# Expert rows added to the residual in DRAM by indirect transfers, in place of gathered rows added on VectorE

## What is computed

```python
h2 = rmsnorm(x, norm2_g[l])
x = x + hier_moe(h2, ...)    # top-1 group of 4, then top-2 experts of the 4 in it
# in hier_moe, for every expert e:  y = y + (silu(t @ w_gate[e]) * (t @ w_up[e]) * gate[:, e]) @ w_down[e]
```

## Time and profile before

| | us |
|---|---|
| median of 3 runs | 1093.71 (1092.78 to 1094.87) |
| the profiled execution | 1096.58 |
| its span, first to last instruction | 1094.3 |
| around the span | 2.3 |
| PE busy | 1034.2 (95%) |
| DVE busy | 549.2 (50%) |
| ACT busy | 291.3 (27%) |
| POOL busy | 191.8 (18%) |

### The profile page before, as it was taken

The page is one execution under the profiler, slowest core; times in us unless marked ns, Lnnn a source line. Parts: engine busy times, 40 slices in busy tenths (PEclk is TensorE's granted clock), DMA queues, the critical chain, the costliest instruction groups (busy, mean ns, idle before and its releaser), DMA issues.

```text
span 1094.3 us, 26585 instructions
## 1 busy us (share of the span) xinstructions
PE 1034.2 (95%) x11288; PEld 765.1 (70%) x11288; DVE 549.2 (50%) x1264; ACT 291.3 (27%) x570; POOL 191.8 (18%) x265
## 2 busy tenths in 40 slices
PE   8999998899999999899989999989999999998894
PEld 7875874587689977586578577646876778764552
DVE  5899996524711111020679999764364112102018
ACT  6225336623000100000342443465230001000013
POOL 3400000000223442322200000000003335332230
PEclk9999999999999999999999999999999999999997
DMA  9652211153999999999934122011569999999993
GB/s 358 209 230 78 77 58 39 39 193 147 394 399 406 402 404 401 405 402 400 345 125 137 53 93 89 20 51 50 202 261 401 403 406 400 404 401 407 396 389 127
DMA packets 85109, 279.07 MB, mean 255 GB/s; under 512 B 12344, under 2 KB 12448, under 8 KB 84976
## 3 DMA queue, kind: packets, MB, share of 16 engines
q1 hardware_dynamic: 69504, 237.60, 56.8%
q0 software_dynamic: 15472, 39.63, 9.8%
HBM read 257.43 MB, written 22.54 MB: 256 GB/s over the span
## 4 chain that ended last, share of the span: by engine, by line
PE 64%; DVE 16%; DMA 10%; issue 3%; ACT 3%; SPq 3%; DVEq 0%; ACTq 0%
PE ps L861 20%; PE ps L901 9%; DVE arena L1620 7%; PE ps L459 7%; PE ps L461 7%; PE ps L460 7%; DMA deep<-in_w_dn 3%; DMA deep<-in_w_gu 3%; SPq L410 3%; DVE w_lo L440 2%; PE ps L906 2%; DMA arena<-in_w_dn 2%; DVE x_sb L1559 2%; DMA arena<-in_w_gu 2%; PE ps L1048 2%
## 5 line engine op out<-in xcount | busy, mean ns | idle before, releaser
L1839 DVE SCALAR_TENSOR_TENSOR arena<-ps,gslot,arena 128x128 f32<-128x128 f32 x88 | 25.7, 345 | 368.1 <-ACT arena L1259 333.2
L861 PE MATMUL ps<-arena 128*32 128x256 f32 x2112 | 129.6, 380 | 6.3 <-DMA arena<-in_w_dn 3.2
L640 POOL DMA_INDIRECT gain<-h_rows,tab x82 | 85.1, 1037 | 231.6 <-DVE arena L1831 188.9
L459 PE MATMUL ps<-a_hi,w_hi 128*128 128x512 f32 (+1 forms) x304 | 122.5, 403 | 3.1 <-DVE w_lo L440 2.1
L460 PE MATMUL ps<-a_lo,w_hi 128*128 128x512 f32 (+1 forms) x304 | 119.3, 392 | 0.0
L461 PE MATMUL ps<-a_hi,w_lo 128*128 128x512 f32 (+1 forms) x304 | 119.2, 392 | 0.0
L861 PEld LDWEIGHTS ps<-arena 128*32 128x32 f32 x2112 | 90.4, 110 | 39.2 <-issue 9.7
L861 PE MATMUL ps<-deep,arena 128*32 128x256 f32 x1824 | 106.6, 379 | 1.0 <-DMA deep<-in_w_dn 1.0
L861 PE MATMUL ps<-raw,arena 128*32 128x256 f32 x1696 | 103.2, 379 | 0.5
L435 ACT ACTIVATE w_hi<-raw 128x1024 fp32r<-128x1024 f32 (+1 forms) x64 | 65.0, 1022 | 131.1 <-PE ps L461 130.9
L1259 ACT ACTIVATE arena<-ps 128x384 f32<-128x384 f32 (+1 forms) x32 | 14.9, 465 | 315.3 <-PE ps L861 248.8
(11 more groups left out here) (266 smaller groups left out, 1511.7 us busy)
## 6 DMA issues: line engine op xcount, KB each, us to landing
arena<-in_w_gu SPq DMA_DIRECT2D x92, 512.0 KB
deep<-in_w_gu SPq DMA_DIRECT2D x84, 512.0 KB
raw<-in_w_gu SPq DMA_DIRECT2D x80, 512.0 KB
raw<-in_w_dn SPq DMA_DIRECT2D x56, 512.0 KB
deep<-in_w_dn SPq DMA_DIRECT2D x44, 512.0 KB
raw<-in_w_in SPq DMA_DIRECT2D x40, 512.0 KB
arena<-in_w_dn SPq DMA_DIRECT2D x28, 512.0 KB
raw<-in_w_out SPq DMA_DIRECT2D x16, 512.0 KB
```

The costliest lines, as they stand in the source:

```text
L459: nc.tensor.matmul(o, lh, rh, start=start, stop=False)
L640: pool.indirect_dma_start(xg[:, s * QC:(s + 1) * QC], None, h2q[l], bass.IndirectOffsetOnAxis(ap=tab[:, s, e:e + 1], axis=0), bounds_check ...
L861: mm = T.matmul(o, rows, piece[:, :, c * P:(c + 1) * P], start=b == 0, stop=b == 7)
L1839: ins = V.scalar_tensor_tensor(out=slu[:, s, :], in0=hidden(e, 1)[:, s, :], scalar=gslot[:, s, e:e + 1], in1=slu[:, s, :], op0=ALU.mult, o ...
```

## The change

The DRAM buffer in slot order is no longer used for the stored places. A DRAM buffer per layer in token order, `xsum`, takes its part. POOL stores each tile of the mixed x into it, ahead of the tile of h2. For each stored place POOL issues an indirect DMA per group of 32 slots (three, or two for a light place), which adds the 128 quarter rows of `ysb` to the rows of `xsum` that `tab` names; an empty slot's index is out of bounds. Before a place's additions it waits until those of the place before have landed. At the end four plain DMAs load the sums over x. The late additions, their eight indirect gathers, the index steps in `extras` and eleven of the twelve zero stores are gone. The places 14 and 15 go as before.

```diff
@@ zero stores, layer 0
-                    for tile in range(1 + EXTRA):
-                        pool.dma_start(yd[ZERO_ROW + tile * P:ZERO_ROW + (tile + 1) * P, :], zeros).then_inc(y_zero, 16)
+                    pool.dma_start(yd[ZERO_ROW:ZERO_ROW + P, :], zeros).then_inc(sums_begun, 16)
@@ mixing phase, for each tile tt
+                    pool.wait_ge(x_mixed, 8 * l + 2 * (tt + 1))
+                    pool.dma_start(xsum[l][tt * P:(tt + 1) * P, :], x[:, tt, :]).then_inc(sums_begun, 16)
                     pool.wait_ge(hrow_set, 4 * k + tt + 1)
                     pool.dma_start(h2d[l][tt * P:(tt + 1) * P, :], hrow[:, tt, :]).then_inc(h2_stored, 16)
@@ def store(e)
                     pool.wait_ge(y_set, STORED * l + e + 1)
-                    rows = yd[FIRST_ROW[e]:FIRST_ROW[e + 1], :].rearrange("(s i) (c n) -> c i s n", i=G, c=4)
-                    for c in range(4):
-                        pool.dma_start(rows[c], ysb[G * c:G * c + G, 0:GROUPS_OF[e] * QC].rearrange("i (s n) -> i s n", n=QC)).then_inc(y_stored, 16)
+                    if e:
+                        pool.wait_ge(y_stored, 16 * stored(l, e))
+                    else:
+                        pool.wait_ge(sums_begun, 16 * (1 + TT * (l + 1)))
+                    for s in range(GROUPS_OF[e]):
+                        pool.indirect_dma_start(xsq[l], bass.IndirectOffsetOnAxis(ap=tab[:, s, e:e + 1], axis=0), ysb[:, s * QC:(s + 1) * QC], None,
+                                                bounds_check=4 * SEQ - 1, oob_is_err=False, compute_op=ALU.add).then_inc(y_stored, 16)
@@ after the last store
-                if l == 0:
-                    pool.wait_ge(y_zero, 16 * (1 + EXTRA))
-                pool.wait_ge(y_stored, 64 * STORED * (l + 1))
+                pool.wait_ge(y_stored, 16 * stored(l, STORED))
                 for tt in range(TT):
-                    for k in range(TOPE):
-                        q = TOPE * tt + k
-                        if q == LATE_FREE:
-                            pool.wait_ge(w_used, (l + 1) * PIECES_L - 8)
-                        pool.indirect_dma_start(late_rows[q], None, yd,
-                                                bass.IndirectOffsetOnAxis(ap=yidx[:, 0, k, tt:tt + 1], axis=0)).then_inc(yc_in[tt], 16)
+                    pool.dma_start(x[:, tt, :], xsum[l][tt * P:(tt + 1) * P, :]).then_inc(x_back[tt], 16)
@@ SP, ahead of the second group of projection weights of layer 1
-                            sp.wait_ge(yc_in[TT - 1], 32 * l)
+                            sp.wait_ge(x_back[TT - 1], 16 * l)
@@ DVE
-            def add_late(l, tt):
-                ve.wait_ge(yc_in[tt], 32 * (l + 1))
-                for k in range(TOPE):
-                    ve.wait_ge(late_add, TOPE * (TT * l + tt) + k)
-                    V.tensor_tensor(x[:, tt, :], late_rows[TOPE * tt + k], x[:, tt, :], ALU.add).then_inc(late_add, 1)
             def sum_ready(l, tt):
-                ve.wait_ge(late_add, TOPE * (TT * l + tt + 1))
+                ve.wait_ge(x_back[tt], 16 * (l + 1))
                 ve.wait_ge(ysum_ready, TT * l + tt + 1)
@@ DVE, extras(l): the twelve steps that made yidx[:, 0] are removed
@@ DVE, end of a layer
                     last_y(l, 0)
-                    add_late(l, 0)
-                    add_late(l, 1)
                     last_y(l, 1)
-                    add_late(l, 2)
-                    add_late(l, 3)
```

More of the change, by code:

```diff
@@ L76 @@
 TURNED = [sum(GROUPS_OF[:p]) for p in range(E + 1)]
-FIRST_ROW = [sum(ROWS_OF[:p]) for p in range(E + 1)]
 EXTRA = 11
@@ L80 @@
 STORED = E - LAST
-ZERO_ROW = FIRST_ROW[STORED]
+ZERO_ROW = 0
 SUM_BANK = (2, 4, 6, 0)
@@ L191, in trunk @@
         warm = sb("warm", [P, 2 + 2 * DEPTH])
-        yidx = sb("yidx", [P, 2, TOPE, TT], I32)
+        yidx = sb("yidx", [P, TOPE, TT], I32)
         e2k = sb("e2k", [P, TOPE, TT])
@@ L208, in trunk @@
         h2q = [rows.rearrange("t (q n) -> (t q) n", q=4) for rows in h2d]
+        xsum = [nc.dram_tensor(f"x_sums{l}", (SEQ, D), F32, kind="Internal").ap() for l in range(DEPTH)]
+        xsq = [rows.rearrange("t (q n) -> (t q) n", q=4) for rows in xsum]
         yd = nc.dram_tensor("y_rows", (OVER_ROW + EXTRA * P, D), F32, kind="Internal").ap()
@@ L261, in trunk @@
         SIDE_MIX, SIDE_ROWS = 6, 10
-        late_rows = [ar(A_ACC, D), ar(A_SQ, D), *(deep[:, d].rearrange("p a n -> p (a n)") for d in (3, 7)),
-                     ar(A_L, D), ar(A_PT, D), hrow[:, TT - 1, :], ar(A_V, D)]
-        LATE_FREE = 5
         at = A_SC
@@ L317, in trunk @@
         conv_tap, pool_d, pw_in = sem("conv_tap"), sem("pool_d"), sem("pw_in")
-        y_zero = sem("y_zero")
+        sums_begun = sem("sums_begun")
         qk_ready, logit_set, exp_set, pt_ready, pt_set, pv_ready, rinv_set, r_ready, o_set = (
@@ L338, in trunk @@
             sem(n) for n in ("lasthot_set", "put_ready", "put_set", "ylast_hi", "ylast_lo"))
-        yc_in = [sem(f"yc_in{tt}") for tt in range(TT)]
-        ysum_ready, late_add = sem("ysum_ready"), sem("late_add")
+        x_back = [sem(f"x_back{tt}") for tt in range(TT)]
+        ysum_ready = sem("ysum_ready")
         x_moe = sem("x_moe")
@@ L490, in gathered, with stored @@
             return sum(s < GROUPS_OF[e] for e in range(1, behind))
+        def stored(l, e):
+            return TURNED[STORED] * l + TURNED[e]
         def gu_bank(e):
@@ L675, in _ @@
                 with pool.If(extra > 0):
-                    pool.wait_ge(late_add, TT * TOPE * (l + 1))
                     pool.wait_ge(over[l].tab_step, TABLES)
@@ L690, in _ @@
                         for tt in range(TT):
-                            pool.indirect_dma_start(x[:, tt, :], None, yd, bass.IndirectOffsetOnAxis(ap=yidx[:, 1, k, tt:tt + 1], axis=0),
+                            pool.indirect_dma_start(x[:, tt, :], None, yd, bass.IndirectOffsetOnAxis(ap=yidx[:, k, tt:tt + 1], axis=0),
                                                     compute_op=ALU.add).then_inc(over[l].xg_in, 16)
@@ L1264, in y_rows @@
                 if l or e:
-                    sc.wait_ge(y_stored, 64 * (STORED * l + e))
+                    sc.wait_ge(y_stored, 16 * stored(l, e))
                 n = GROUPS_OF[e]
@@ L1745, in extras @@
                     link(V.scalar_tensor_tensor(out=R["ex"], in0=R["count"], scalar=float(q), in1=R["ex"], op0=ALU.is_gt, op1=ALU.add))
[L1746 to L1753, removed]
                 link(V.tensor_tensor_scan(R["cum"], cst[:, C_ONE:C_ONE + E], R["ex"], 0.0, ALU.mult, ALU.add))
-                link(V.scalar_tensor_tensor(out=R["c2"], in0=R["k2"], scalar=float(CAP), in1=R["c2"], op0=ALU.is_lt, op1=ALU.mult))
                 V.tensor_tensor(first_of[:], R["cum"], R["ex"], ALU.subtract)
                 V.tensor_copy(ovx[:, EXTRA:EXTRA + 1], R["cum"][:, E - 1:E])
-                link(V.scalar_tensor_tensor(out=R["c2"], in0=R["b2"], scalar=float(-ZERO_ROW), in1=R["c2"], op0=ALU.add, op1=ALU.mult))
-                V.tensor_scalar(yidx[:, 0], R["c2"], float(ZERO_ROW), None, ALU.add)
                 link(V.tensor_tensor(R["cmp"], R["cum"].unsqueeze(1).to_broadcast([P, EXTRA, E]),
@@ L1802, in over_rows @@
                 step(V.scalar_tensor_tensor(out=R["d2"], in0=R["b2"], scalar=float(OVER_ROW - ZERO_ROW - E * P), in1=R["d2"], op0=ALU.add, op1=ALU.mult))
-                V.tensor_scalar(yidx[:, 1], R["d2"], float(ZERO_ROW), None, ALU.add)
+                V.tensor_scalar(yidx[:], R["d2"], float(ZERO_ROW), None, ALU.add)
                 for k in range(TOPE):
@@ L1927, in _ @@
                 if l == 0:
-                    ve.wait_ge(y_zero, 16 * (1 + EXTRA))
+                    ve.wait_ge(sums_begun, 16)
                 for v, (h, b) in enumerate(DOTS):
@@ L2061, in _ @@
                     last_y(l, 1)
-                    for tt in range(TT):
-                        add_late(l, tt)
                     O = over[l]
```

## The result

The changed kernel takes **1103.2 us** in the median (four runs, 1101.7 to 1105.3), the kernel before in the same comparison 1094.3. The ratio is 1.0076, with an interval from 1.0058 to 1.0093: slower by 0.6 to 0.9%.

A forecast was written before the change was run, and what follows sets the result against it. The weight stream was taken to bound the expert stages, late additions a layer's end. Per layer 6.9 + 1.3 - 3.9 = +4.3 us, for two layers +8.6, took the median from 1093.7 to 1102.3 us; range 1083 to 1130.

The forecast's parts named there:

- The stage is bound by the weight stream: Expert stages: DMA engines never rest, PE close behind; added DMA work moves the stage's end by as much.
- the stage absorbs it: Rival, expert stage: unseen DMA slack hides the 8 us and only the ends change, 1085.9 us; chance 0.10.
- The additions, +6.9 us a layer: Expert stage: additions cost two transfers of filled rows, 7.8 MB, 19.3 us, against 12.4 us for the stores before.
- The upper end, +12.3 us: Expert stage, a layer: two transfers with no saving from empty slots, 24.7 us; as total 1113.1 us.
- The end of a layer, -3.9 us a layer: Layer's end: without the four late additions behind the last residue the first sum comes 3.9 us sooner, together -7.8 us.
- The x rows, +1.3 us a layer: Four new x stores a layer: three cost nothing, the fourth, 0.52 MB, falls where the DMA share is full.
- POOL and ACT, nothing: Expert stage: POOL's longer issues and ACT's wait for slower additions cost nothing, with some 14 us of room.
- The signs for PE: Expert stage: if right, PE's waits for weights rise by about 8 us a layer and the stage ends later by that.
- x comes back in time: Last step: the plain loads are in x at 531, 7 us before needed at 537.9; cost nothing.
- Zeros and indices, nothing: 5.8 MB less zero stores and index steps ending 2 us sooner, before a DMA-bound stage: nothing gained.
- The read is hidden: Rival, expert stage: an addition costs only its written rows, -5.3 us a layer, 1083.1 us; chance 0.13.
- Additions far dearer: Rival, expert stage: engines stand between read and write; three transfers +14.0 a layer, 1121.7 us, four 1141; chance 0.22.

The follow-up runs named there:

- e4: The kernel before with every store of a stored place made twice, the second into a buffer nobody reads: 1116.3 us, 1.0196 of before.
- e1: The changed kernel with its 76 indirect additions made plain indirect writes of the same rows: 1085.3 us, 0.9928 of before.
- e2: The changed kernel with four plain stores a place instead of the additions: 1660 us, the overflow path ran, so only layer 0 can be read.
- e6: The changed kernel without the stores of the mixed x, sum buffers zeroed once at the start: 1101.4 us, 1.0079 of before.
- e5: The changed kernel with two `ysb` buffers in turn for the light places, so ACT need not wait for the place before: 1104.4 us, 1.0102 of before.
- e10: The kernel before with tile 0's late additions ahead of last_y of place 14 and tile 3's made by POOL: 1092.6 us against 1095.1, 0.9977.

## Why the prediction was right

The sum was 1102.3 us, the measurement 1103.2 (8.6 us more than before, against 8.9), and the sign and the mechanism held. That the number is so close is luck in part: the filled share, the price, the part of the added work that the stage passes on and the end of a layer were each off, and the errors nearly cancel. Point by point:

- **The stage is bound by the weight stream.** Right, though not by the full amount: 12.4 us of DMA work lengthened the stages by 10.3 and 11.9 us (e4), and 13 us by 10.1 and 9.0 (e1). The rival "the stage absorbs it" is out.
- **The additions, +6.9 us a layer.** The sum came out nearly right from terms that were each off. The filled share was put at 78%, from the gathers of a window; e1 moved 3.50 MB, 70% of the 4.98 (the addition packets of the changed kernel's layer 0 give 3.56 MB, 71%). The price was put at two transfers at 403 GB/s. At 153 GB/s an addition is 2.6 of these, and a layer's 3.50 MB hold the engines for 23 us and not 19.3. Against this stands that the stage did not pass on all of the added time (e1). The stages grew by 9.0 and 7.8 us where 6.9 + 1.3 = 8.2 was forecast.
- **The page on additions.** In the Trainium skill, Collectives: The Full Stack, section "The bandwidth ceiling: the fold count and why AG ≠ RS ≠ AR", an addition reads two sources for one write and runs at 1/1.93 of a copy's rate. The trace agrees that an addition is dearer by about that much: it measures 1/2.35 for rows of 1 KB, and 1/2.1 between packets of one size. That the second read is the cause isn't shown here.
- **The upper end, +12.3 us.** Whether empty slots save less because they lie on the same engines isn't shown: it wasn't tried, and the stages leave no room for the full +12.3.
- **The end of a layer, -3.9 us a layer: mis-sized, it is -4.9 and -5.0.** The step that was wrong is that "the four additions before last_y(15) lie beside PE's last products and cost nothing now". They held up last_y(15) by 1.8 us (16.4 against 14.6 us, in every run without them). The part behind the residue was 3.1 us and not 3.9, since the first sum is ready 1.8 us after the residue's end, where 1.0 had been read off PE's rows.
- **The x rows, +1.3 us a layer.** Not contradicted: e2 gives 1.6 and e6 1.7 and 0.5 us, but the stages vary as much from trace to trace, so the term is not told apart from nothing.
- **POOL and ACT, nothing.** The outcome was right, a step in it wrong: ACT's room of 14 us was not there, and ACT waited 38.9 us for landings. e5 took most of that away and nothing was gained. The signs for PE were off too: its waits for weights rose by 6.4 and not 8 us in the first trace, and with the plain scatter of e1 they were as long while the stage was 10 us shorter.
- **x comes back in time.** Right, with less room than forecast. The loads were issued at 531.6 us and took up to 10.3 us to land; the first sum started at 546.2, and PE released it.
- **Zeros and indices, nothing.** Nothing is seen of them: the stage of layer 0 starts at 278.10 us, before at 278.04.
- **The read is hidden** (1083.1 us): out, by e1, where a scatter of the same rows takes the kernel to 1085.3, near that rival's time. **Additions far dearer**: out, at 2.6 transfers and stages 7 to 9 us longer.

## What to carry to other kernels

A DMA that adds in DRAM takes work from DVE, and its bytes cost the DMA engines more than twice the time of copied ones (2.35 times here). Beside a weight stream that fills these engines it lost 8.9 us; where they have time it may pay, which no run here tried. A full DMA share with falling GB/s (387 at 1.05, where it was 403 at 1.03) was here the sign of dearer transfers; the stage's end, not the waits, says what they cost. Before an operation at a stage's end is called hidden, look at whether it holds its engine when the last input comes, and what would be late next without it: here that was a landing that no wait of the first trace named.

## What the hardware showed that was not expected

- An indirect addition of 128 rows of 1 KB takes POOL 1.57 us to issue, the plain scatter of e1 0.97 to 1.03, an indirect gather of as many 1.04 to 1.05, a gather of 4 KB rows 0.94.
- Added rows went at 153 GB/s of engine time, scattered rows at 359. Each added row of 1 KB was a packet of its own, 101 ns, while copies of four rows shared a packet of 168 ns.
- A float32 addition of 128 x 1024 takes POOL 2.4 to 3.3 us and DVE 1.22; one of DVE's beside it took 3.3 us.
- Three of the kernels (e1, e2, e5) took 13.2 to 13.9 us from the first sum to the next norm's first split, where before and after took 11.4 and e10 12.5; some 2 us of the totals of e1 and e5 are this and not the stage. In e1 and e5 the granted clock over these us was 0.87, in the changed kernel 1.00, but before it was 0.85 with no such loss; what decides it stays open.
